# Hybrid layers of a two-block network on one core: output turned in another chunk order and partly inside the last projection, entry splits placed ahead of the norms, roots in place of log and exp

## The chip, the cores and the metric

One NeuronCore of a Trainium2 chip runs the whole program in a single launch. The metric is device time in microseconds, the median of several executions. The same program is timed before and after the change on the same inputs. Engine names are those of the profile: PE is TensorE (PEld its weight loads), DVE VectorE, ACT ScalarE, SP the engine whose queue issues the weight DMAs.

## The reference

Two blocks of two layers each, on 256 tokens of width 2048, in fp32. The first block (a pool and convolution mixer, then a gated linear recurrence) is the same before and after. The change is in the second block, whose layer is, cut to what matters here:

```python
h = rms_norm_2(x, pre_w)
proj = h @ w_in                                  # 2048 -> 5952 columns
a_q, a_k, a_v, a_g, b_q, b_k, b_v, b_g, c_q, c_kv, c_kr, c_g = jnp.split(proj, offsets, axis=-1)
...
y_a = diff_attention(qa, ka, va, lam, subln_w, lam_init)       # 4 heads, each normalised (subln_w)
...
y_b = sliding_window_attention(qb, kb, vb, sinks)              # 16 heads of 64, 2 key heads
...
qc = (rms_norm_2(c_q, q_norm_w) @ w_uq).reshape(B, S, MLA_HEADS, MLA_NOPE_DIM + MLA_ROPE_DIM)
...
kvc = (rms_norm_2(c_kv, kv_norm_w) @ w_ukv).reshape(B, S, MLA_HEADS, MLA_NOPE_DIM + MLA_V_DIM)
...
y_c = causal_attention(qc, kc, vc, (MLA_NOPE_DIM + MLA_ROPE_DIM) ** -0.5)
y = jnp.concatenate([y_a, y_b, y_c], axis=-1) * jax.nn.silu(jnp.concatenate([a_g, b_g, c_g], axis=-1))
out = y @ w_out
return x + rms_norm_2(out, post_w)
```

y has 2048 columns: 512 of y_a, 1024 of y_b, 512 of y_c. `c_q` and `c_kv` (the ranks) are normalised over their 512 columns before the second projection.

## The kernel before

**Weights and splits.** Every fp32 product is made as three fp32r matmuls (`three`): high x high, high x low, low x high. Weights come in chunks of 1 MB (four k-tiles of 128 rows by 512 columns) that SP loads into four `raw` buffers in program order. For each half chunk ScalarE writes the high part (`hi`, line 577, `wh`) and VectorE the low part (`lo`, line 1794, `wl`); there are two `wh`/`wl` slots, so a half chunk can be split once TensorE has used the half two chunks earlier (`s_used`). TensorE waits for the low part (`s_lo`) at each half.

**Entry of a hybrid layer** (`enter` on ACT and DVE, `enter_project` on PE). x is normalised only by a scale per token (`rsh`) that is applied later. Chunks 0 and 1 are multiplied per token tile while the second tile is turned, then chunk 2 and chunk 3 follow. On ACT the order around it is: high parts of h, chunk 2, the square of token tile 0 (`x_square`, lines 953 and 954), chunk 3, the square of tile 1, six DMAs of small parameters (lines 986 to 988), chunk 4. On DVE it is: low parts, chunk 2, low parts, a reciprocal of `rsh` and the scaled rotary tables, chunk 3.

**Projection.** 16 blocks (`BLOCKS`) make 52 chunks, that is half chunks i = 4 to 103 in the loops of all three engines. The table `AFTER` says after which half chunk each further step runs: `move` takes a finished block out of its two PSUM banks (0, 1 or 2, 3 in turn), `norm` turns and scales the rank blocks cq and ckv, `turn` transposes rotated heads, and `score`, `flip`, `weigh` are the attention of one of 14 pairs (2 of kind m for c, 8 of kind b, 4 heads of kind a). A half chunk is 12 matmuls. Each engine walks the table in its own order; DVE does kind a's `weigh` two half chunks late, ACT one.
- `move cq` and `move ckv` (ACT lines 1006 to 1009): square both tiles with accumulation, copy the block, then `Ln` and `Exp` of the sums give the root's inverse; DVE (line 2453) makes scaled diagonals for `norm`.
- `move ag`, `move cg`: ACT writes the sigmoid (line 1027), DVE the product (lines 2493 to 2498).
- `weigh` of kind a: ACT squares (1070), `Ln` and `Exp` (1072, 1073); DVE scales and gates (2576, 2580).

**Turning y and the output projection.** y (`Yt`, tokens in partitions) is turned by `turn_y(g)`, four transposes for a pair g of 128-column tiles into one of banks 4 to 7 (line 1758). ACT copies the pair to `hTh` (1102), DVE subtracts for `hTl` (2626), which frees the bank. After the last half chunk PE turns pairs 0 to 3, and pairs 4 to 7 ahead of k = 0, 2, 4, 6 of output block 0 (`y_ahead`). An output block n has four chunks c (k-tiles 4c to 4c+3), two token tiles, so 24 matmuls a chunk; blocks use banks 0, 1 and 2, 3 in turn. Pairs 0 and 1 hold the a heads, 2 to 5 the b heads, 6 and 7 the c heads, which need the cg product. After the last turned pair ACT issues the DMA of the post-norm row and four of the residual (lines 1108, 726), and DVE waits for that row before it splits output chunk 2.

Of the kernel before, what the change touches and what calls it, by code (L numbers as in the profile page):

```python
# [7 lines left out]
F32 = mybir.dt.float32  # L8
# [6 lines left out]
P = 128  # L15
# [204 lines left out]
for _h, _name in ((48, "bg0"), (56, "bq1"), (64, "bg1"), (72, "aq"), (80, "ak"), (88, "av"), (96, "ag")):  # L220
    AFTER.setdefault(_h, []).append(f"move {_name}")
# [4 lines left out]
YT = KT // 2  # L226
TWO_PI = 6.283185307179586
# [6 lines left out]
def first_block_and_hybrid(nc, a):  # L234

    ctx = ExitStack()
    with ctx:
# [231 lines left out]
        def _(sp):  # L469
# [69 lines left out]
            for L in range(2):  # L539
# [16 lines left out]
                for i in range(16):  # L556
                    ch = st.chunk("hyb", L, NPROJ + i)
                    load(ch, [(slot4(ch), one(layer(w_out2[:, i % 4], L)[:, :, :, (i // 4) * BLK:(i // 4 + 1) * BLK]))])
# [8 lines left out]
        def _(act):  # L567
# [374 lines left out]
            def enter(L, last, SQ):  # L942
# [27 lines left out]
                hyb_split(L, 2)  # L970
                x_square(0)
                hyb_split(L, 3)
# [7 lines left out]
            def hyb_layer(L):  # L980
# [4 lines left out]
                for i, n in enumerate(("q1", "k1", "q2", "k2")):  # L985
                    act.dma_start(LQ[:, i, :], a[f"diff_lambda_{n}_2"][bass.ds(L, 1), :].rearrange("o n -> (o n)").partition_broadcast(P)).then_inc(s_lp, 16)
                act.dma_start(SUB, a["diff_subln_w_2"][bass.ds(L, 1), :].rearrange("o n -> (o n)").partition_broadcast(P)).then_inc(s_lp, 16)
                act.dma_start(SNK, a["sink_logits_2"][bass.ds(L, 1), :].rearrange("o n -> (o n)").partition_broadcast(P)).then_inc(s_lp, 16)
                act.wait_ge(s_save, L * 32 + 64)

# [8 lines left out]
                def move(name, i):  # L999
                    b, _ = done(i)  # L1000
                    if name in ("cq", "ckv"):
# [6 lines left out]
                        step(nc.scalar.activation(qrs[:, 2 * v:2 * v + 2], qss[:, 2 * v:2 * v + 2], ACT.Ln, scale=1.0 / 512, bias=eps)).done()  # L1008
                        nc.scalar.activation(qrs[:, 2 * v:2 * v + 2], qrs[:, 2 * v:2 * v + 2], ACT.Exp, scale=-0.5).then_inc(s_qs, 1)
# [10 lines left out]
                    elif name[1] == "g":  # L1020
# [7 lines left out]
                        ins.then_inc(s_gx, 1)  # L1028

# [35 lines left out]
                def weigh(n):  # L1065
                    kind, h = PAIRS[n]
                    if kind == "a":
# [4 lines left out]
                        step(nc.scalar.activation(ors, oss, ACT.Ln, scale=1.0 / P, bias=C("eps")[:, 1:2])).done()  # L1072
                        nc.scalar.activation(ors, ors, ACT.Exp, scale=-0.5).then_inc(s_os, 1)
# [16 lines left out]

                hyb_split(L, 4, (0,))
                for i in range(6, 2 * NPROJ):
# [6 lines left out]
                hi(st.chunk("hyb", L, NPROJ))  # L1099
                for g in range(YT):  # L1100
                    act.wait_ge(s_yt, count(YT, g + 1))
                    nc.scalar.activation(hTh[:, 2 * g:2 * g + 2, 0:SEQ], ps[:, 4 + g % 4, :].rearrange("p (a b) -> p a b", a=2),
                                         ACT.Copy).then_inc(s_yth, 1)
                    if g == 3:
                        hi(st.chunk("hyb", L, NPROJ + 1))
# [5 lines left out]
                for m in range(2, 16):  # L1111
# [16 lines left out]
        def _(pe):  # L1128
# [160 lines left out]
            def out_block(chunks, T, bank, before=None, after=None):  # L1289

                for c, ch in enumerate(chunks):
                    for t in range(4):
                        if t % 2 == 0:
                            pe.wait_ge(s_lo, ch.half(t // 2))
                        k = 4 * c + t
                        if before:
                            before(k)
                        for m in range(T):
# [3 lines left out]
                                        k == 0, k == KT - 1, False)  # L1302
# [297 lines left out]
            def hyb_layer(L):  # L1600
# [137 lines left out]

                enter_project(L)
# [11 lines left out]
                def turn_y(g):  # L1751
# [932 lines left out]
```

## Time and profile before

| | us |
|---|---|
| median of 3 runs | 2792.46 |
| lowest, highest | 2789.76, 2798.06 |
| the profiled execution: its own time | 2791.23 |
| its span on the core | 2789.4 |

The mean granted clock of TensorE over the span is 0.989 of full speed. The hybrid layers run from about 1877 us to the end: the first layer's entry at 1877 to 1908, its last score at 2205, its output projection to 2341, then the second layer in the same form. In the tables of the profile, a line "[x <-ENGINE ...]" gives the idle time of the instruction's engine just before it and the instruction that ended the wait. Matmul ends are modelled, so starts are the safer reading.

### The profile page before, as it was taken

What the parts mean: (1) busy time and instruction counts of PE and PEld (TensorE: products, weight loads), DVE (VectorE), ACT (ScalarE), POOL (GpSimd) and SP (SyncE); (2) the same over time, 40 slices, a digit from 0 to 9 for tenths busy, and PEclk for the clock granted to TensorE, in tenths of its full rate; (3) what the DMA queues carried; (4) which work ended last, traced back from release to release, by engine and by line L of the source; (5) the groups of instructions that cost most, each with busy time, mean ns of one, the idle gap of its engine ahead of it and who ended that gap; (6) DMA issues with size and microseconds to landing.
All of it is one profiled execution on the core that took longest, in us unless ns stands there. A gap on an engine that the chain in (4) does not pass through costs nothing.

```text
span 2789.4 us, 36467 instructions
## 1 busy us (share of the span) xinstructions
PE 2668.9 (96%) x13605; PEld 2199.2 (79%) x13605; DVE 1898.5 (68%) x2677; ACT 1273.1 (46%) x2017; POOL 0.2 (0%) x4
## 2 busy tenths in 40 slices
PE   5999999999999899999999999998999989999988
PEld 2667778888788788888888888777888777878867
DVE  5765577887887677677677677856566555656654
ACT  6653321222322755345345345456455646545563
POOL 0000000000000000000000000000000000000000
PEclk9999999999999999999999999999999999999999
DMA  8764455665556333323323323455644465544453
GB/s 309 263 223 154 158 168 156 211 197 168 179 211 203 122 97 101 113 87 101 113 87 101 113 86 107 146 172 177 188 133 154 136 207 183 172 151 151 151 181 136
DMA packets 406588, 437.16 MB, mean 157 GB/s; under 512 B 22718, under 2 KB 286536, under 8 KB 404936
## 3 DMA queue, kind: packets, MB, share of 16 engines
q1 hardware_dynamic: 397760, 408.99, 45.9%
q10 hardware_dynamic: 8712, 26.59, 2.6%
q8 instruction: 76, 1.25, 0.2%
q14 instruction: 40, 0.33, 0.0%
HBM read 427.14 MB, written 8.39 MB: 156 GB/s over the span
## 4 chain that ended last, share of the span: by engine, by line
PE 82%; DVE 9%; ACT 5%; issue 2%; DMA 1%; ACTq 0%; DVEq 0%; SPq 0%
PE ps L1132 14%; PE ps L1133 14%; PE ps L1134 14%; PE ps L1135 9%; PE ps L1137 9%; PE ps L1136 9%; DVE wl L1794 3%; DVE acc L1865 2%; ACT wh L577 1%; PE ps L1442 1%; PE ps L1156 1%; PE ps L1158 1%; PE ps L1463 1%; PE ps L1447 1%; PE ps L1735 1%
## 5 line engine op out<-in xcount | busy, mean ns | idle before, releaser
L1794 DVE TENSOR_TENSOR wl<-raw,wh 128x1024 fp32r<-128x1024 f32 (+2 forms) x784 | 821.3, 1077 | 465.4 <-ACT wh L577 453.6
L577 ACT ACTIVATE wh<-raw 128x1024 fp32r<-128x1024 f32 (+2 forms) x784 | 714.4, 943 | 828.2 <-PE ps L1134 472.3
L1132 PE MATMUL ps<-hTh,wh 128*128 128x512 f32 (+1 forms) x2124 | 777.9, 366 | 19.6 <-DVE wl L1794 16.1
L1133 PE MATMUL ps<-hTl,wh 128*128 128x512 f32 (+1 forms) x2124 | 766.8, 361 | 0.0
L1134 PE MATMUL ps<-hTh,wl 128*128 128x512 f32 (+1 forms) x2124 | 765.6, 360 | 0.0
L1135 PE MATMUL ps<-wh,hTh 128*128 128x512 f32 (+1 forms) x1440 | 575.6, 400 | 25.3 <-DVE wl L1794 18.8
L1137 PE MATMUL ps<-wh,hTl 128*128 128x512 f32 (+1 forms) x1440 | 558.5, 388 | 0.0
L1136 PE MATMUL ps<-wl,hTh 128*128 128x512 f32 (+1 forms) x1440 | 557.7, 387 | 0.0
L1132 PEld LDWEIGHTS ps<-hTh,wh 128*128 128x128 f32 x2124 | 401.9, 189 | 89.9 <-DVE wl L1794 9.8
L1133 PEld LDWEIGHTS ps<-hTl,wh 128*128 128x128 f32 x2124 | 401.8, 189 | 61.6 <-issue 0.5
L1134 PEld LDWEIGHTS ps<-hTh,wl 128*128 128x128 f32 x2124 | 401.0, 189 | 62.0
L1135 PEld LDWEIGHTS ps<-wh,hTh 128*128 128x128 f32 x1440 | 272.8, 189 | 88.3 <-DVE wl L1794 26.7
L1137 PEld LDWEIGHTS ps<-wh,hTl 128*128 128x128 f32 x1440 | 272.3, 189 | 55.9
L1136 PEld LDWEIGHTS ps<-wl,hTh 128*128 128x128 f32 x1440 | 273.3, 190 | 51.2 <-issue 1.7
L1865 DVE SCALAR_TENSOR_TENSOR acc<-raw,small,acc 128x1024 f32<-128x1024 f32 x180 | 217.4, 1276 | 0.0
L1053 ACT ACTIVATE arena<-arena,small 128x256 f32<-128x256 f32 (+1 forms) x112 | 49.6, 444 | 128.9 <-DVE small L2537 69.5
L2253 DVE RECIPROCAL arena<-arena 128x512 f32<-128x512 f32 x32 | 107.0, 3345 | 0.0
L1156 PE MATMUL ps<-wh,s 128*66 128x512 f32 x192 | 84.5, 440 | 23.2 <-DVE wl L1794 17.8
L1158 PE MATMUL ps<-wl,s 128*66 128x512 f32 x192 | 81.1, 422 | 0.0
L2288 DVE SCALAR_TENSOR_TENSOR arena<-arena,small,ps 128x128 f32<-128x128 f32 x192 | 66.8, 348 | 6.9
L1156 PEld LDWEIGHTS ps<-wh,s 128*66 128x66 f32 x192 | 28.4, 148 | 52.6 <-DVE wl L1794 19.0
L2281 DVE COPY arena<-ps 128x128 f32<-128x128 f32 x32 | 9.2, 287 | 76.0 <-PE ps L1442 76.0
(296 smaller groups left out, 2029.2 us busy)
## 6 DMA issues: line engine op xcount, KB each, us to landing
raw<-in_ada_w_dram SPq DMA_DIRECT2D x96, 1024.0 KB, 5.3
raw<-in_w_in_dram SPq DMA_DIRECT2D x88, 1024.0 KB, 5.1
raw<-in_od_w_in_dram SPq DMA_DIRECT2D x256, 320.0 KB, 3.5
raw<-in_ev_w_in_dram SPq DMA_DIRECT2D x192, 256.0 KB, 3.9
raw<-in_w_out_dram SPq DMA_DIRECT2D x32, 1024.0 KB, 5.0
raw<-in_ev_w_out_dram SPq DMA_DIRECT2D x16, 1024.0 KB, 5.1
raw<-in_od_w_out_dram SPq DMA_DIRECT2D x16, 1024.0 KB, 5.1
x_save<-arena ACTq DMA_DIRECT2D x6, 1024.0 KB, 5.5
```

What stands on the lines that cost most here:

```text
L577: nc.scalar.activation(wh[:, ch.spl, part], raw[:, ch.raw, part], ACT.Copy).then_inc(s_hi, 1)
L1132: nc.tensor.matmul(out, w_h, x_h, start=first, stop=False, skip_group_check=True)
L1133: nc.tensor.matmul(out, w_h, x_l, start=False, stop=False, skip_group_check=True)
L1134: return nc.tensor.matmul(out, w_l, x_h, start=False, stop=last, skip_group_check=True)
L1135: nc.tensor.matmul(out, x_h, w_h, start=first, stop=False, skip_group_check=True)
L1136: nc.tensor.matmul(out, x_h, w_l, start=False, stop=False, skip_group_check=True)
L1137: return nc.tensor.matmul(out, x_l, w_h, start=False, stop=last, skip_group_check=True)
L1156: nc.tensor.matmul(psA(n), s4[:, 4 * k:4 * k + MS], wh[:, ch.spl, t * BLK:(t + 1) * BLK], start=(k == 0), stop=False, skip_group_check=True)
L1158: ins = nc.tensor.matmul(psA(n), s4[:, 4 * k:4 * k + MS], wl[:, ch.spl, t * BLK:(t + 1) * BLK], start=False, stop=(k == KT - 1), skip_grou ...
L1794: nc.vector.tensor_tensor(wl[:, ch.spl, part], raw[:, ch.raw, part], wh[:, ch.spl, part].bitcast(F32), ALU.subtract).then_inc(s_lo, 1)
L1865: ins = nc.vector.scalar_tensor_tensor(out=acc[:, v, :], in0=w, scalar=silc[:, k:k + 1], in1=acc[:, v, :], op0=ALU.mult, op1=ALU.add)
L2253: step(nc.vector.reciprocal(R[:, d, :], R[:, d, :])).done()
```

## The change

All of it is in the two hybrid layers.
- **Order of y.** Output block 0 takes its chunks in the order `Y_ORDER` = 1, 2, 0, 3 (b heads, b heads, a heads, c heads); SP loads them in that order. `Y_PAIR` and `Y_BANK` give the pair and the bank of the n-th turn. Turn 0 runs after half chunk 101, turn 1 after 102, turns 2 to 7 ahead of k-steps 1, 2, 4, 5, 7, 8 of output block 0 (`Y_AT`). ACT and DVE take their parts of turn 0 inside the loop, and split output chunk 2 ahead of turns 6 and 7. DVE's wait for the post-norm row moves from chunk 2 to behind the split of chunk 5.
- **Gate ag** moves after half chunk 98 (ACT) and 99 (DVE), not 96.
- **Entry.** Both halves of chunk 3 are split ahead of both squares on ACT and ahead of the reciprocal on DVE; the six parameter DMAs and the wait for the saved x come behind the first half of chunk 4.
- **Roots.** `Ln` and `Exp` become one `Sqrt` on ACT and a reciprocal on DVE, for the ranks and for the a heads. For the ranks the root runs one half chunk later (`root`), DVE's part two half chunks later.

```diff
-for _h, _name in (..., (96, "ag")):
+for _h, _name in (..., (98, "ag")):
...
+Y_ORDER = (1, 2, 0, 3)
+Y_PAIR = [2 * c + h for c in Y_ORDER for h in range(2)]
+Y_BANK = (7, 6, 4, 5)
+Y_AT = {1: 2, 2: 3, 4: 4, 5: 5, 7: 6, 8: 7}
...
@@ ACT, enter
                 hyb_split(L, 2)
+                hyb_split(L, 3)
                 x_square(0)
-                hyb_split(L, 3)
                 x_square(1).then_inc(s_sqp, 1)
...
@@ ACT, hyb_layer
-                        step(nc.scalar.activation(qrs[:, 2 * v:2 * v + 2], qss[:, 2 * v:2 * v + 2], ACT.Ln, scale=1.0 / 512, bias=eps)).done()
-                        nc.scalar.activation(qrs[:, 2 * v:2 * v + 2], qrs[:, 2 * v:2 * v + 2], ACT.Exp, scale=-0.5).then_inc(s_qs, 1)
...
+                def root(v):
+                    nc.scalar.activation(qrs[:, 2 * v:2 * v + 2], qss[:, 2 * v:2 * v + 2], ACT.Sqrt, scale=1.0 / 512, bias=eps).then_inc(s_qs, 1)
...
-                        step(nc.scalar.activation(ors, oss, ACT.Ln, scale=1.0 / P, bias=C("eps")[:, 1:2])).done()
-                        nc.scalar.activation(ors, ors, ACT.Exp, scale=-0.5).then_inc(s_os, 1)
+                        nc.scalar.activation(ors, oss, ACT.Sqrt, scale=1.0 / P, bias=C("eps")[:, 1:2]).then_inc(s_os, 1)
...
+                    if i in (8, 16):
+                        root(i // 8 - 1)
...
@@ PE, hyb_layer
+                def turn_y(n):
+                    g = Y_PAIR[n]
+                    if n == 0:
+                        pe.wait_ge(s_45, count(len(USE45), USE45.index("weigh 9") + 1))
+                        pe.wait_ge(s_67, count(len(USE67), USE67.index("turn ak") + 1))
+                    elif n == 1:
+                        pe.wait_ge(s_67, count(len(USE67), len(USE67)))
+                    elif n == 2:
+                        pe.wait_ge(s_45, count(len(USE45), len(USE45)))
+                    elif n == 6:
+                        moved("cg")
+                    if n >= 4:
+                        pe.wait_ge(s_ytl, count(YT, n - 3))
...
+                    if i == 2 * NPROJ - 3:
+                        turn_y(0)
+                    if i == 2 * NPROJ - 2:
+                        turn_y(1)
...
@@ DVE, enter
+                split(3)
                 dve.wait_ge(s_sqp, L * 9 + 25)
                 step(nc.vector.reciprocal(rsh, rsh)).done()
...
                 dve.wait_ge(s_rsh, L + 1)
-                split(3)
...
@@ DVE, hyb_layer
+                        step(nc.vector.reciprocal(qrs[:, 2 * v:2 * v + 2], qrs[:, 2 * v:2 * v + 2])).done()
...
+                        step(nc.vector.reciprocal(ors, ors)).done()
...
+                    for what, late in (("move cq", 2), ("move ckv", 2), ("move ag", 1)):
+                        if what in AFTER.get(i - late, []):
+                            move(what.split()[1], (i - late - 1) // 2)
...
+                    if i == 2 * NPROJ - 3:
+                        lo(st.chunk("hyb", L, NPROJ))
+                        low_turned(0)
+                low_turned(1)
                 lo(st.chunk("hyb", L, NPROJ + 1))
-                for g in range(4, 6):
-                    low_turned(g)
+                low_turned(2)
+                low_turned(3)
                 after(2 * NPROJ - 1)
-                for g in range(6, YT):
-                    low_turned(g)
-                dve.wait_ge(s_gl, L * 16 + 16)
-                for m in range(2, 18):
+                low_turned(4)
+                low_turned(5)
+                lo(st.chunk("hyb", L, NPROJ + 2))
+                low_turned(6)
+                low_turned(7)
+                for m in range(3, 18):
...
+                        if n == 0:
+                            dve.wait_ge(s_gl, L * 16 + 16)
```

ACT at a hybrid layer's entry, before; line 577 is a half chunk's high part, 953 a square.

```order
L577 ACTIVATE wh<-raw 128x1024 x2
L953 ACTIVATE arena,small<-arena 128x2048
L954 ACTIVATE small<-small,cst 128x1
L577 ACTIVATE wh<-raw 128x1024 x2
L953 ACTIVATE arena,small<-arena 128x2048
L954 ACTIVATE small<-small,cst 128x1
```

The same place in the change (577 is now 581, 953 is 957).

```order
L581 ACTIVATE wh<-raw 128x1024 x4
L957 ACTIVATE arena,small<-arena 128x2048
L958 ACTIVATE small<-small,cst 128x1
L957 ACTIVATE arena,small<-arena 128x2048
L958 ACTIVATE small<-small,cst 128x1
L581 ACTIVATE wh<-raw 128x1024
```

Chunk 3's two halves have moved ahead of both squares, and the parameter DMAs that followed the second square now follow one half of chunk 4.

DVE from the ag product to the last score and on, before; 1794 is a half chunk's low part, 2493 to 2498 the product, 2524 and 2526 the read of the last score, 2576 the weighing.

```order
L2576 SCALAR_TENSOR_TENSOR arena<-ps,small 128x128 x2
L2493 SCALAR_TENSOR_TENSOR arena<-ps,small,arena 128x512 x2
L2497 COPY arena<-arena 128x2x256
L2498 TENSOR_TENSOR arena<-arena 128x2x256
L1794 TENSOR_TENSOR wl<-raw,wh 128x1024
L2524 SCALAR_TENSOR_TENSOR arena<-ps,cst 128x2x256
L2526 SCALAR_TENSOR_TENSOR arena<-ps,cst 128x2x128
```

And in the change (1794 is now 1823, 2493 is 2523, 2524 is 2554, 2576 is 2607, 2603 the new reciprocal).

```order
L2607 SCALAR_TENSOR_TENSOR arena<-ps,small 128x128 x2
L1823 TENSOR_TENSOR wl<-raw,wh 128x1024
L2554 SCALAR_TENSOR_TENSOR arena<-ps,cst 128x2x256
L2556 SCALAR_TENSOR_TENSOR arena<-ps,cst 128x2x128
...
L1823 TENSOR_TENSOR wl<-raw,wh 128x1024
L2523 SCALAR_TENSOR_TENSOR arena<-ps,small,arena 128x512 x2
L2527 COPY arena<-arena 128x2x256
L2528 TENSOR_TENSOR arena<-arena 128x2x256
L1823 TENSOR_TENSOR wl<-raw,wh 128x1024
L2603 RECIPROCAL small<-small 128x2
L2607 SCALAR_TENSOR_TENSOR arena<-ps,small 128x128
```

The read of the last score has moved ahead of the product, and the product now stands directly ahead of the weighing of head 2.

PE's turns (line 1758) and their waits, before; each `x3` or `x15` row completes a turn.

```order
L1758 MATMUL ps<-cst,arena 128x128 [waits block_moved0,banks67_read,banks45_read]
L1758 MATMUL ps<-cst,arena 128x128 x15
L1758 MATMUL ps<-cst,arena 128x128 [waits y_turned_low,low_ready]
L1758 MATMUL ps<-cst,arena 128x128 x3
L1135 MATMUL ps<-wh,hTh 128x512 [waits y_turned_low]
```

In the change (1758 is now 1775, 1735 is 1755, 1135 is 1155); the first two turns stand on either side of the last head's weighing.

```order
L1775 MATMUL ps<-cst,arena 128x128 [waits banks67_read,banks45_read]
L1775 MATMUL ps<-cst,arena 128x128 x3
L1155 MATMUL ps<-wh,hTh 128x512 [waits low_ready]
...
L1755 MATMUL ps<-arena 128x128 [waits block_moved1,banks67_read,banks45_read]
...
L1775 MATMUL ps<-cst,arena 128x128 [waits banks67_read]
L1775 MATMUL ps<-cst,arena 128x128 x3
L1155 MATMUL ps<-wh,hTh 128x512 [waits low_ready]
...
L1155 MATMUL ps<-wh,hTh 128x512 [waits y_turned_low,low_ready,block_moved0]
...
L1775 MATMUL ps<-cst,arena 128x128 [waits banks45_read]
```

Matmuls stand between the turns, where the 16 transposes stood in one piece before.

## Rows read from the trace of the kernel before

**Rows 1.** page, part 1: busy time, share of the span, instructions
```profile
PE 2668.9 (96%) x13605; PEld 2199.2 (79%) x13605; DVE 1898.5 (68%) x2677; ACT 1273.1 (46%) x2017; POOL 0.2 (0%) x4
```

**Rows 2.** windows view: span; busy us (count) of PE, PEld, DVE, ACT, POOL; clock, DMA
```profile
1905.10:1923.30 18.20, 18.17 (x73) 14.69 (x74) 8.98 (x16) 12.10 (x17) 0.00 (x0) 0.91 0.41 120
2204.90:2267.70 62.80, 50.47 (x223) 40.41 (x224) 33.55 (x48) 33.37 (x54) 0.00 (x0) 0.92 0.50 174
2657.90:2716.30 58.40, 47.05 (x223) 37.94 (x224) 33.55 (x48) 33.38 (x54) 0.00 (x0) 0.97 0.53 186
```

**Rows 3.** timeline of PE, first hybrid layer's turn: start, us, instruction, [idle before <-releaser]
```profile
2210.73 0.49 PE L1735 MATMUL ps<-arena 128*128 128x128 f32 x2 [1.89 <-DVE arena L2526]
...
2230.46 1.97 PE L1758 MATMUL ps<-cst,arena 128*128 128x128 f32 x16 [2.49 <-DVE arena L2580]
2235.68 0.88 PE L1758 MATMUL ps<-cst,arena 128*128 128x128 f32 x4 [3.25 <-DVE hTl L2626]
...
2245.16 0.63 PE L1758 MATMUL ps<-cst,arena 128*128 128x128 f32 x4 [1.29 <-issue]
...
2255.13 0.50 PE L1135 MATMUL ps<-wh,hTh 128*128 128x512 f32 x1 [3.38 <-DVE wl L1794]
```

**Rows 4.** timeline of PE, second hybrid layer's turn
```profile
2663.74 0.49 PE L1735 MATMUL ps<-arena 128*128 128x128 f32 x2 [1.93 <-DVE arena L2526]
...
2682.59 0.44 PE L1758 MATMUL ps<-cst,arena 128*128 128x128 f32 x2 [2.49 <-DVE arena L2580]
...
2687.81 0.63 PE L1758 MATMUL ps<-cst,arena 128*128 128x128 f32 x4 [1.94 <-DVE hTl L2626]
...
2695.68 0.52 PE L1758 MATMUL ps<-cst,arena 128*128 128x128 f32 x3 [1.28 <-issue]
...
2705.37 0.51 PE L1135 MATMUL ps<-wh,hTh 128*128 128x512 f32 x1 [3.11 <-DVE wl L1794]
```

**Rows 5.** timeline of PE: matmuls at either clock, and four transposes between matmuls
```profile
2212.77 0.63 PE L1136 MATMUL ps<-wl,hTh 128*128 128x512 f32 x1
...
2240.05 0.40 PE L1136 MATMUL ps<-wl,hTh 128*128 128x512 f32 x1
2240.28 0.40 PE L1137 MATMUL ps<-wh,hTl 128*128 128x512 f32 x1
2240.52 0.60 PE L1758 MATMUL ps<-cst,arena 128*128 128x128 f32 x4
2240.88 0.48 PE L1135 MATMUL ps<-wh,hTh 128*128 128x512 f32 x1
```

**Rows 6.** timeline of PE, entry and block kvr of the first hybrid layer
```profile
1905.13 0.80 PE L1135 MATMUL ps<-wh,hTh 128*128 128x512 f32 x1 [2.45 <-DVE wl L1794]
...
1943.43 0.41 PE L1135 MATMUL ps<-wh,hTh 128*128 128x320 f32 x1 [2.07 <-DVE wl L1794]
```

**Rows 7.** timeline of ACT, first hybrid layer's entry
```profile
1896.28 2.09 ACT L953 ACTIVATE arena<-arena 128x2048 f32<-128x2048 f32 x1
...
1898.69 1.99 ACT L577 ACTIVATE wh<-raw 128x1024 fp32r<-128x1024 f32 x2
...
1905.50 1.06 ACT L577 ACTIVATE wh<-raw 128x1024 fp32r<-128x1024 f32 x1 [2.60 <-issue]
```

**Rows 8.** timeline of ACT, block ckv of the first hybrid layer
```profile
1938.78 1.28 ACT L1008 ACT_TABLE_LOAD   x1
...
1941.79 0.72 ACT L577 ACTIVATE wh<-raw 128x640 fp32r<-128x640 f32 x1
```

**Rows 9.** timeline of DVE, first hybrid layer's turn
```profile
2206.14 0.75 DVE L2493 SCALAR_TENSOR_TENSOR arena<-ps,small,arena 128x512 f32<-128x512 f32 x1 [1.27 <-ACT arena L1027]
...
2209.67 0.68 DVE L2524 SCALAR_TENSOR_TENSOR arena<-ps,cst 128x512 f32<-128x512 f32 x1
...
2239.51 0.68 DVE L2626 TENSOR_TENSOR hTl<-ps,hTh 128x512 fp32r<-128x512 f32 x1
...
2253.85 4.63 DVE L1794 TENSOR_TENSOR wl<-raw,wh 128x1024 fp32r<-128x1024 f32 x4 [3.50 <-DMA arena<-in_post_norm_w_dram]
```

More of the change, by code:

```diff
@@ L557, in _ @@
                     ch = st.chunk("hyb", L, NPROJ + i)
-                    load(ch, [(slot4(ch), one(layer(w_out2[:, i % 4], L)[:, :, :, (i // 4) * BLK:(i // 4 + 1) * BLK]))])
+                    load(ch, [(slot4(ch), one(layer(w_out2[:, Y_ORDER[i] if i < 4 else i % 4], L)[:, :, :, (i // 4) * BLK:(i // 4 + 1) * BLK]))])
             for u in range(4):
@@ L1098, in hyb_layer @@
                     after(i)
[L1099 to L1105, printed above, removed]
+                    if i == 2 * NPROJ - 3:
+                        hi(st.chunk("hyb", L, NPROJ))
+                        high_turned(0)
+                high_turned(1)
+                hi(st.chunk("hyb", L, NPROJ + 1))
+                high_turned(2)
+                high_turned(3)
+                after(2 * NPROJ - 1)
+                high_turned(4)
+                high_turned(5)
+                hi(st.chunk("hyb", L, NPROJ + 2))
+                high_turned(6)
+                high_turned(7)
                 act.wait_ge(s_yt, count(YT, YT))
@@ L1110, in hyb_layer @@
                     load_x(u, x_rows, XBN)
-                for m in range(2, 16):
+                for m in range(3, 16):
                     hi(st.chunk("hyb", L, NPROJ + m))
@@ L1287, in gate_rows, with out_block @@
                 nc.tensor.matmul(ps[:, 6 + r % 2, :], ones, gate_block(r), start=True, stop=True).then_inc(s_gb, 1)
-            def out_block(chunks, T, bank, before=None, after=None):
+            def out_block(chunks, T, bank, before=None, after=None, order=range(4)):
                 for c, ch in enumerate(chunks):
@@ L1294, in out_block @@
                             pe.wait_ge(s_lo, ch.half(t // 2))
-                        k = 4 * c + t
+                        k = 4 * order[c] + t
                         if before:
-                            before(k)
+                            before(4 * c + t)
                         for m in range(T):
@@ L1777, in hyb_layer @@
                         free_banks(L * 3 + 6, n)
-                    out_block([st.chunk("hyb", L, NPROJ + 4 * n + c) for c in range(2 if n == 3 else 4)], 2, 2 * (n % 2), y_ahead if n == 0 else None)
+                    out_block([st.chunk("hyb", L, NPROJ + 4 * n + c) for c in range(2 if n == 3 else 4)], 2, 2 * (n % 2), y_ahead if n == 0 else None, order=range(4) if n else Y_ORDER)
                 last_chunks([st.chunk("hyb", L, NPROJ + 14), st.chunk("hyb", L, NPROJ + 15)], 1 if L == 0 else None)
@@ L2602, in after @@
                         if verb == "move":
-                            move(arg, (i - 1) // 2)
+                            if arg not in ("cq", "ckv", "ag"):
+                                move(arg, (i - 1) // 2)
                         elif verb == "norm":
```

67 lines of the change are left out of this document (32 added, 35 removed).

## The prediction

> **What bounds the kernel now.** I read four views in this order. The page's busy times say which engine the span follows: TensorE is busy for 2668.9 of 2789.4 us, VectorE and ScalarE for 68% and 46% [rows 1]. So only time in which TensorE stands still, or runs at the lower clock, can be won; shorter work on ScalarE or VectorE is worth nothing unless TensorE waits for it. The TensorE timeline then gives each wait inside the two hybrid layers, with the instruction that ended it [rows 3, 4, 6]. The windows view sums the stretches around those waits [rows 2]; it holds exactly the same 223 TensorE instructions in both layers. The timelines of ScalarE and VectorE say what was in front of the late instruction [rows 7 to 9]. Everything before the first hybrid layer is untouched and costs or gives nothing.
>
> In the stretch from the last score to the end of output block 0 (I call it the turn), TensorE waited 1.89 + 2.49 + 3.25 + 1.29 + 3.38 = 12.30 us in the first layer [rows 3] and 1.93 + 2.49 + 1.94 + 1.28 + 3.11 = 10.75 us in the second [rows 4]. At the start of each layer it waited 2.45 us for chunk 3 of the entry and 2.07 us in block kvr [rows 6]; the second layer shows the same two waits with the same lengths.
>
> The clock comes on top. A 512-column matmul takes 0.40 us at the upper level, 2.4 GHz, where the next follows after 0.23 us, and 0.63 us at the lower, 1.2 GHz [rows 5]. The granted clock was 0.92 and 0.97 over the two turns and 0.91 over the 18.20 us behind the first entry's wait [rows 2]. The share missing from 1 is time lost: 0.08 x 62.80 = 5.0 us, 0.03 x 58.40 = 1.8 us, 0.09 x 18.20 = 1.6 us. The last is one stretch, so a stretch costs about 1.6 to 1.7 us and the first turn held three.
>
> **Entry.** Chunk 3's high split on ScalarE began at 1898.69, behind a square of 2.41 us that began at 1896.28 [rows 7]; its low split on VectorE stood behind a reciprocal that needs the second square, done at 1905.50 - 2.60 = 1902.90. Both now go first. The high split can start at about 1896.3 and both halves end at 1898.3; VectorE then has 4.4 us for its own part (1.16 us a half, a quarter of 4.63 [rows 9]) and eight small low parts until TensorE wants it at 1905.13 - 2.45 = 1902.68. I take the 2.45 us as gone. Late next is chunk 4: two squares take ScalarE to 1903.1, half a chunk to 1904.1, the six DMA issues with their waits 2.60 us, the second half to 1907.7, its low part to 1908.9. TensorE wants it 36 matmuls of 0.23 us after 1902.68, at 1911.0. Slack 2.1 us; without that cover it would cost what the squares cost, 2.4 us.
>
> **Ranks.** In block ckv, ScalarE loaded a table for Ln, ran it, loaded one for Exp, ran it, and only then split a half chunk of kvr: 1938.78 to 1941.79, 3.01 us [rows 8]. The change runs the square root after that split, so the split comes 3.0 us earlier against a wait of 2.07: gone. What is late next is the normalisation's diagonal, which now stands behind a square root with one load of 1.28 us, a reciprocal and one more VectorE step; by the same durations it ends within 0.3 us of when TensorE wants it, and I keep 0.3 us a layer for it. The rows show a load before Ln and one before Exp. The Trainium skill's page "ScalarE: Activation LUTs", section "Table sets", says the opposite for the old pair and speaks against the new one: Ln and Exp share a set (one load), Exp and Sqrt do not (two). By that rule the old pair was the cheaper, and the ckv gain would be 1.3 us a layer smaller. The rows decide, and rows 8 have both loads. Per attention head of kind a the old code had two loads (Ln, Exp) and the new one has two (Sqrt, Exp), but one of them now falls where ScalarE waits for the row maximum: no cost on TensorE, counted as nothing. The reciprocals added on VectorE (six a layer, a few elements each) are hidden by its 32% idle time.
>
> **Gate ag.** VectorE began the ag product at 2206.14 and could read the last score only at 2209.67 [rows 9]; TensorE's weighing of head 2 waited 1.89 us for that read [rows 3]. Two or three half chunks later the product no longer stands there, and the read can come up to 3.5 us earlier. The wait goes. In its place the read of head 2's weighing becomes late, behind the product; I keep 0.5 us a layer.
>
> **Turns.** Before, 16 transposes stood behind the last head, then each trip (copy on ScalarE, 0.68 us subtraction on VectorE [rows 9], transposes into the freed bank) was seen: 2.49 + 3.25 + 1.29 us. Now pairs 0 and 1 are turned while 24 matmuls of the last projection (5.5 us) are still to come, and each later pair at least three k-steps, 18 matmuls or 4.1 us, before its use. Eight turns of four transposes stay in TensorE's stream at 0.36 us each, from 2240.52 to 2240.88 [rows 5]. The wait of 3.38 us ended with the arrival of the post-norm row, for which VectorE waited 3.50 us before splitting output chunk 2 [rows 9]; that wait now stands behind chunk 5. Next late is chunk 3: after the last turn ScalarE has a copy, five DMA issues (about the 2.60 us of rows 7) and a half split, VectorE 1.16 us, in all some 5.4 us against 24 matmuls of 0.23, 5.5 us. Just covered. The order of chunks and of their loads changes no size and no count.
>
> **Sum.** From below, a turn gives its waits and its clock: 12.30 + 5.0 = 17.3 us and 10.75 + 1.8 = 12.5 us. From above, the stretch at full pace is 168 matmuls of 0.23, 8 turns of 0.36 and 23 small matmuls of about 0.09, that is 38.6 + 2.9 + 2.1 = 43.6 us; 62.80 - 43.6 = 19.2 and 58.40 - 43.6 = 14.8 us. I take the middle, 18.2 and 13.7, less 0.5 each: 17.7 + 13.2 = 30.9 us. Entries and ranks: 2 x (2.45 + 2.07) + 1.6 - 0.6 = 10.1 us. Together 41 us. The profiled execution took 2791.2 us (1.8 around its span) and stands 1.2 us under the median: 2791.2 - 41 + 1.2 = **2751.4 us**.
>
> **Rivals.**
> - Cover too thin at the third output chunk, **chance 0.17**. VectorE's 33.55 us of work in the turn then fill 33.55 / 45.1 = 74% of it, with the product of cg and the last pairs in one queue. If the 3.38 and 3.11 us come back, each with one stretch at the lower clock, 6.5 + 3.4 = 9.9 us of the gain stay out: 2761. For it speaks the slack of under 0.5 us; against it that the arrival which made the wait is no longer waited for.
> - The clock still falls although the waits are gone, **0.08**: 8.4 us back, 2760. Against it: the second layer had waits of 1.28 to 3.11 us and lost only 1.8 us.
> - Turning drops the clock, **0.04**. A mechanism of this kernel: each of 16 turned pairs is followed by one stretch of 1.7 us loss, 27 us, 2779. The matmuls on both sides of the transposes at 2240.52 are at the upper level [rows 5], which speaks against it. The Trainium skill's "TensorE: Matmul & The Clock Gate", Part 4, says that transposes do not count as activity in the way matmuls do; by that rule spreading them into the stream could invite this.
> - The trip is seen eight times instead of once, **0.02**. If ScalarE or VectorE reach each pair so late that the 3.25 us of rows 3 stand before every use, that is 16 x 3.25 = 52 us against the 23 us of waits before, with no clock won: 29 - 10 = 19 us slower, 2811. It turns into a loss from (23 + 10) / 16 = 2.1 us per pair on. Against it: 4.1 us of matmuls between turn and use.
> - The entry's moves only push the wait from chunk 3 to chunk 4 or 5, **0.05**: 10 us of gain gone, 2761.
>
> **How the numbers follow.** My case has 0.64, with its own range 2744 to 2757: its lower end is the upper bounds (19.2 + 14.8 + 10.7 = 44.7 us), the small waits for heads that I left alone and the 2.7 us by which runs fall under the median. The range of 8 in 10 reaches up over the three rivals near 2761 with their spread of runs: 2743 to 2767. A measurement tells 0.3%, 8.4 us, from no change. Every case named but the slower one ends faster by more than that; I give up 0.03 of theirs for what I have not thought of: faster 0.95, within 0.3% 0.03, slower 0.02.
>
> **What would show it.** In the changed profile, TensorE's waits at the two entries' chunk 3, in block kvr, before the head 2 weighing, before the turns and before the third output chunk should each be under 0.6 us; the granted clock over the turn should be 1.00 and the turn 45 us long in both layers; ScalarE should show ten table loads fewer in the hybrid layers. I am wrong if a wait over 1 us stands at chunk 4 or 5 of the entry, at the ckv diagonal, at the weighing of head 3, or at output chunk 3, or if the clock is under 0.97 in the turn.

## The result, and the profile after

The changed kernel takes **2746.06 us** (median of 4 runs, 2743.45 to 2747.09); the kernel before took 2795.01 us beside it (4 runs, 2789.76 to 2798.06). The ratio is 0.983, 95% interval 0.9814 to 0.9846: faster. A second comparison gave 2746.35 us and 0.9828 (0.9813 to 0.9843). The forecast was 2751.4 us in a range of 2743 to 2767: inside the range, with 5.3 us too small a gain. That counts from the 2792.46 us before the change; the runs of the kernel before beside it lie 2.6 us higher.

The busy times of the page, in the columns of [rows 1]:

```profile
PE 2656.7 (97%) x13605; PEld 2194.6 (80%) x13605; DVE 1900.9 (69%) x2689; ACT 1258.7 (46%) x1995; POOL 0.2 (0%) x4
```

The count of TensorE's instructions is the same, and it is busy 12.2 us less although it does the same work. Most of that is time at the lower clock that has gone (in the clock record about 8.5 us in the hybrid layers and 1.7 us ahead of them); the rest I can't place, since a matmul's busy time is modelled. The span fell by 44.1 us, from 2789.4 to 2745.3.

The windows of after are from the first entry to the last score of the first layer, then the two turns; the last two answer to the turns in [rows 2]:

```profile
1877.30:2198.10 320.80, 316.42 (x1658) 262.77 (x1656) 206.56 (x371) 178.28 (x323) 0.00 (x0) 1.00 0.51 162
2198.13:2242.80 44.67, 44.67 (x224) 37.14 (x224) 32.60 (x50) 28.73 (x49) 0.00 (x0) 1.00 0.56 198
2627.60:2672.30 44.70, 44.70 (x225) 37.18 (x225) 32.57 (x50) 28.65 (x49) 0.00 (x0) 1.00 0.55 200
```

Both turns are 44.7 us at a clock of 1.00, with TensorE busy from end to end: 62.80 - 44.67 = 18.1 us and 58.40 - 44.70 = 13.7 us won, 31.8 in all.

The waits view of TensorE over the two hybrid layers (engine, line, waited for: us in total, times, longest), first of the kernel before, from 1876 us on:

```profile
PE ps L1135 <- DVE wl L1794: 17.5, 8, 3.4
PE ps L1735 <- DVE arena L2526: 5.8, 6, 1.9
PE ps L1758 <- DVE hTl L2626: 5.2, 2, 3.2
PE ps L1758 <- DVE arena L2580: 5.0, 2, 2.5
PE ps L1758 <- issue: 2.6, 2, 1.3
PE ps L1135 <- DVE hTl L2377: 2.3, 2, 1.1
```

and all that this view shows of the changed kernel, from 1877 us on:

```profile
PE ps L1155 <- DVE hTl L2406: 2.3, 2, 1.1
PE ps L1755 <- DVE arena L2556: 2.0, 4, 0.5
PE ps L1155 <- DVE wl L1823: 1.9, 2, 1.0
PE ps L1575 <- DVE arena L2169: 1.7, 4, 0.5
PE ps L1690 <- DVE arena L2483: 0.5, 2, 0.2
PE ps L1741 <- DVE small L2578: 0.4, 2, 0.2
```

Before, with the smaller groups of that view, the waits are 42 us; after, 8.8 us. The three groups of line 1758, the turns' own, are gone entirely, and of the eight waits for a weight split two are left, 0.96 and 0.98 us at chunk 2 of each entry. The rest of the gain is the clock: before, five stretches at the lower clock stood in the hybrid layers (one in the first entry, three in the first turn, one in the second), each of 3.4 us in the record and, by the terms of the prediction, worth about 1.7 us; after, there is none. (Both kernels have one more behind their last matmul, where it costs TensorE nothing.) 33.4 + 5 x 1.7 = 41.9 us. The hybrid layers (from their first transposes to the end of the span, called the **hybrid part** below) went from 912.5 to 867.9 us, that is 44.6. The missing 2.7 us I don't have one by one; a wait's length is counted from the modelled end of the matmul ahead, 0.40 us after its start, while at full pace the next begins after 0.23 us [rows 5], and 18 fewer waits (34 before, 16 after) at up to 0.17 us each are room enough for it.

### The profile page after: what moved, and what is told of

Its sections match the earlier page's. It is cut to its first block, busy times and chain, and to the rows that moved or that the text cites. A ratio compares the mean times of both kernels' runs of the same rounds, so it can differ in the third digit from the quotient of the medians.

```text
span 2745.3 us, 36471 instructions
## 1 busy us (share of the span) xinstructions
PE 2656.7 (97%) x13605; PEld 2194.6 (80%) x13605; DVE 1900.9 (69%) x2689; ACT 1258.7 (46%) x1995; POOL 0.2 (0%) x4
## 4 chain that ended last, share of the span: by engine, by line
PE 85%; DVE 8%; ACT 3%; issue 2%; DMA 1%; ACTq 0%; DVEq 0%; SPq 0%
PE ps L1152 14%; PE ps L1153 14%; PE ps L1154 14%; PE ps L1155 10%; PE ps L1157 10%; PE ps L1156 10%; DVE wl L1823 3%; DVE acc L1894 2%; PE ps L1462 1%; PE ps L1176 1%; PE ps L1178 1%; PE ps L1483 1%; ACT wh L581 1%; PE ps L1755 1%; PE ps L1467 1%
```

## The experiments

Each edit is against the changed kernel, except the first. The number I compare is the hybrid part of the profiled execution, since what stands ahead of it is the same code and still took from 1875.2 to 1878.3 us in these profiles, and 1881.4 us in one. The changed kernel has 867.9 us in both of its profiles, the kernel before 912.5 in its only one. Where stretches at the lower clock fall in the hybrid layers the number holds for that execution alone, by steps of 1.7 us: the runs of the kernel before spread from 2786.91 to 2799.64 us with clocks of 0.985 to 0.991, those of the changed kernel from 2743.45 to 2747.09 us.

### The entry alone, in the kernel before

```diff
                 hyb_split(L, 2)
-                x_square(0)
                 hyb_split(L, 3)
+                x_square(0)
                 x_square(1).then_inc(s_sqp, 1)
...
+                split(3)
                 dve.wait_ge(s_sqp, L * 9 + 25)
...
                 dve.wait_ge(s_rsh, L + 1)
-                split(3)
```

> The kernel before with only the entry's order changed: chunk 3 split ahead of both squares on ScalarE and ahead of the reciprocal on VectorE; the six parameter DMAs stay where they were. Theory (each wait is worth its own length, and nothing takes its place): the 2.45 us wait for chunk 3 is gone in both layers and with it the lower-clock stretch behind the first, so 2 x 2.45 + 1.6 = 6.5 us less than before, and the 2.07 us in block kvr stays. Rival (the wait only moves): a wait of 1 to 2.5 us appears at chunk 4 or 5, because the squares and the DMA issues (2.60 us) now stand directly ahead of chunk 4, and the total is within 2 us of before.

Measured: 2788.54 us, ratio 0.9985 (0.9975 to 0.9995); hybrid part 910.1, 2.4 us less than before. By this pair of profiles it is **a miss** for my theory; the medians of 10 and 13 runs say 4.2 us (by the interval 1.4 to 7.0), which leaves the 6.5 us open. Both waits of 2.45 us are gone, but 0.44 and 0.46 us came at the first half of chunk 4 (the squares and, in this kernel, the parameter DMAs too stand ahead of it), so the sum of waits fell by 4.35 us and not by 4.9. And this profile has six lower stretches, where that of before has five. The timeline of TensorE at block kvr of the first hybrid layer, before:

```profile
1943.68 0.31 PE L1136 MATMUL ps<-wl,hTh 128*128 128x320 f32 x1
1943.82 0.31 PE L1137 MATMUL ps<-wh,hTl 128*128 128x320 f32 x1
1943.97 0.31 PE L1135 MATMUL ps<-wh,hTh 128*128 128x320 f32 x1
```

The wait ahead of them is 2.07 us [rows 6]. In this experiment it is 2.07 us too, and the windows view of the 9 us behind it, first and second hybrid layer, is:

```profile
1938.31:1947.31 9.00, 9.00 (x54) 9.00 (x55) 5.54 (x12) 4.00 (x8) 0.00 (x0) 0.81 0.71 235
2386.80:2395.80 9.00, 9.00 (x54) 9.00 (x55) 5.60 (x12) 4.06 (x9) 0.00 (x0) 0.81 0.71 233
```

The same 9 us before:

```profile
1943.43:1952.43 9.00, 9.00 (x65) 9.00 (x66) 7.14 (x14) 5.08 (x9) 0.00 (x0) 1.00 0.69 236
```

So the wait of 2.07 us, which cost nothing beyond its length in the profile of before, cost 0.19 x 9 = 1.7 us more in either layer here. The stretch in the first entry is gone, and the turns have four between them, so the balance is one more: 4.35 - 1.7 = 2.65 us is what is left, against 2.4 in the hybrid part. That the removed wait moved the stretch onto the next is not shown. With one profile of each kernel, another execution of the same kernel could have shown it elsewhere; the next experiment has such a case within one program.

### The entry as before, in the changed kernel

```diff
                 hyb_split(L, 2)
-                hyb_split(L, 3)
                 x_square(0)
+                hyb_split(L, 3)
...
-                hyb_split(L, 4, (0,))
...
                 act.wait_ge(s_save, L * 32 + 64)
+                hyb_split(L, 4, (0,))
...
-                split(3)
                 dve.wait_ge(s_sqp, L * 9 + 25)
...
                 dve.wait_ge(s_rsh, L + 1)
+                split(3)
```

> The changed kernel with the entry's order as before (chunk 3 behind the first square on ScalarE and behind the reciprocal on VectorE, the six parameter DMAs ahead of chunk 4); turns, gate and roots as changed. In the kernel before, the same edit alone gave only about 2 us over the hybrid layers where 6.5 were expected, because lower-clock stretches fell elsewhere. Theory (a wait is worth its length, and the clock comes on top by chance): 2.45 us of wait twice, and one lower-clock stretch or none or two: 4.9 to 8.2 us over the changed kernel. Rival (the entry's order is worth only the 2 us that its run alone showed): under 3 us over.

Measured: 2752.75 us, 0.9852 (0.9835 to 0.987); hybrid part 875.1, 7.2 us over the changed kernel's profile beside it, within the 4.9 to 8.2 expected; the medians, 2752.75 and 2746.35, differ by 6.4. The waits of 2.45 and 2.46 us are back. TensorE behind each of them, windows view:

```profile
1903.46:1912.46 9.00, 9.00 (x39) 7.43 (x40) 4.66 (x4) 6.19 (x9) 0.00 (x0) 1.00 0.66 205
2335.77:2344.77 9.00, 9.00 (x33) 7.30 (x34) 4.67 (x4) 4.67 (x8) 0.00 (x0) 0.82 0.64 206
```

Practically the same wait in the same program: once the clock stays at 2.4 GHz, once it falls to 1.2 GHz for a stretch. In the kernel before, the same wait of 2.45 us was followed by a stretch in the first layer and by none in the second. So a stretch belongs to no wait for good. The entry is worth 6 to 7 us in the changed kernel; in the kernel before it gave 2.4 us by the profiles and 4.2 us by the medians, and these don't tell whether it is worth less there.

### The turns and output chunks as before

```diff
-Y_ORDER = (1, 2, 0, 3)
+Y_ORDER = (0, 1, 2, 3)
...
-Y_BANK = (7, 6, 4, 5)
+Y_BANK = (4, 5, 6, 7)
...
                 moved("ag")
+                for g in range(4):
+                    turn_y(g)
```

(with ACT's and DVE's parts, the loads and the wait for the post-norm row back in their old places; entry, roots and gate stay changed)

> The changed kernel with y turned as before (natural chunk order, 16 transposes behind the last projection, the wait for the post-norm row ahead of output chunk 2); entry, roots and gate ag as changed. Theory: the waits 2.49 + 3.25 + 1.29 + 3.38 us come back in the first layer and 2.49 + 1.94 + 1.28 + 3.11 us in the second, some shorter by the 1.3 us of a table load that the last head no longer has, with one to three lower-clock stretches of 1.7 us: 18 to 24 us over the changed kernel. Rival (the gain of the turn comes from the roots and gate ag, which put the last head earlier): under 8 us over the changed kernel.

Measured: 2772.0 us, 0.9931 (0.9912 to 0.9949); hybrid part 892.1, 24.2 us over the changed kernel, at the upper end of the 18 to 24 expected. The waits come back at the trip and at the third output chunk, in the timeline of TensorE:

```profile
2223.44 1.09 PE L1772 MATMUL ps<-cst,arena 128*128 128x128 f32 x4 [3.54 <-DVE hTl L2653]
...
2232.83 0.63 PE L1772 MATMUL ps<-cst,arena 128*128 128x128 f32 x4 [1.29 <-issue]
...
2242.54 0.50 PE L1149 MATMUL ps<-wh,hTh 128*128 128x512 f32 x1 [3.12 <-DVE wl L1808]
```

The second layer has the same three, 3.54, 1.29 and 2.89 us. These are 15.7 us of waits. The clock is low four times, once for twice the usual length, so as long as in five stretches: 15.7 + 5 x 1.7 = 24.2. The wait of 2.49 us behind the last head [rows 3], which I also expected, did not come back; what removed it I did not try apart. The turns and the output chunks carry more than half of the whole gain, and nothing of the ag wait is in it.

### The order of chunks without the overlap

```diff
-                    if i == 2 * NPROJ - 3:
-                        turn_y(0)
-                    if i == 2 * NPROJ - 2:
-                        turn_y(1)
...
+                turn_y(0)
+                turn_y(1)
                 moved("ag")
```

(ACT's and DVE's parts of turn 0 likewise come behind the loop)

> The changed kernel with turns 0 and 1 behind the last half chunk instead of inside the last projection; the chunk order 1, 2, 0, 3 and the later turns stay. Theory (two things make the turn free: chunk order, which takes the last head and gate cg off the path, and the overlap, which hides the first trip): one trip shows per layer, ScalarE 0.6 and VectorE 0.7 us for a pair and the queues ahead of them, 2 to 4 us a layer, 4 to 8 us in all, with at most one lower-clock stretch a layer more. Rival (order alone does it): under 1 us. Rival (overlap alone does it): over 15 us.

Measured: 2749.3 us, 0.9844 (0.9828 to 0.9861); hybrid part 870.6, only 2.6 us over the changed kernel where 4 to 8 were expected: **a miss in size**. There is one new wait a layer, and no lower stretch:

```profile
2218.32 1.04 PE L1775 MATMUL ps<-cst,arena 128*128 128x128 f32 x8
2220.43 0.47 PE L1155 MATMUL ps<-wh,hTh 128*128 128x512 f32 x1 [1.07 <-DVE hTl L2652]
```

So of the 24.2 us of the run above, the two turns inside the last projection carry 2.6. The other 21.6 go to what this kernel keeps: the new order of chunks (b heads first, whose y is ready before the last head), the turns spread between k-steps, the third output chunk split ahead of the last pairs, and the moved wait for the row, of which only the last was tried by itself, below.

### The wait for the post-norm row back

```diff
                 low_turned(7)
+                dve.wait_ge(s_gl, L * 16 + 16)
                 for m in range(3, 18):
...
-                        if n == 0:
-                            dve.wait_ge(s_gl, L * 16 + 16)
```

> The changed kernel with VectorE's wait for the post-norm row back directly behind the last turn, ahead of output chunk 3 (it stood behind chunk 5). Theory (the row arrives 4.8 us after its issue, some 1.2 us after the split could begin): a wait of 0.7 to 1.3 us at output chunk 3 in each layer, none elsewhere, 1.4 to 2.6 us in all. Rival (the arrival was the whole of the 3.38 us before): about 3 us a layer.

Measured: one run of 2752.82 us; hybrid part 875.7, 7.8 us more. **A miss in size**: 1.4 to 2.6 us were expected. VectorE's timeline at the split of the third output chunk, in this kernel:

```profile
2236.96 4.63 DVE L1823 TENSOR_TENSOR wl<-raw,wh 128x1024 fp32r<-128x1024 f32 x4 [5.55 <-DMA arena<-in_post_norm_w_dram]
```

and in the changed kernel:

```profile
2235.81 4.63 DVE L1823 TENSOR_TENSOR wl<-raw,wh 128x1024 fp32r<-128x1024 f32 x4 [2.35 <-ACT wh L581]
```

TensorE waits 2.71 and 2.86 us at that chunk, the second time with a lower stretch (clock 0.81 over the next 9 us). 5.57 + 1.7 = 7.3 of the 7.8 us. That is three times what I had expected, since I reckoned with the landing time of before. The tile view of the row gives this time; before:

```profile
DMA to landing us min/median/max: 4.5/4.7/4.8
```

in this experiment:

```profile
DMA to landing us min/median/max: 6.8/6.9/7.0
```

The changed kernel itself has 6.9 to 7.0 us too, so it is not this edit that made the landing longer. The row is the same transfer in all three; it takes 2.2 us longer to land than before. The kernel before and the changed one differ in what moves beside it (the output chunks' loads now run into it: DMA share of the turn 0.55 and 0.56, before 0.50 and 0.53 [rows 2]); that this is the cause was not tried by itself. Had the change left this wait where it was, most of the 9.9 us of the rival with the third output chunk would have come true.

### How thin the cover at the third output chunk is

```diff
                     load_x(u, x_rows, XBN)
+                for _ in range(6):
+                    step(nc.scalar.activation(small[:, 506:507], eps, ACT.Copy)).done()
                 for m in range(3, 16):
```

> The changed kernel with six chained tiny copies on ScalarE (about 0.2 us each, 1.2 us in all) ahead of output chunk 3's split. Theory (chunk 3 is covered by 0.3 us only): a wait of 0.7 to 1.2 us appears at output chunk 3 in each layer. Rival (the cover is larger than the starts show): no wait.

Measured: one run of 2750.09 us; hybrid part 870.4, 2.4 us more. The timeline of ScalarE and of TensorE in this kernel:

```profile
2235.29 1.38 ACT L1132 ACTIVATE small<-cst 128x1 f32<-128x1 f32 x6 [1.98 <-issue]
2236.70 3.90 ACT L581 ACTIVATE wh<-raw 128x1024 fp32r<-128x1024 f32 x4
```

```profile
2239.07 0.50 PE L1157 MATMUL ps<-wh,hTh 128*128 128x512 f32 x1 [0.92 <-DVE wl L1825]
```

A delay of 1.41 us on ScalarE becomes a wait of 0.92 us in the first layer and 0.89 in the second, within the expected 0.7 to 1.2. The cover was 0.5 us by the recorded waits, 0.2 by the 2.4 / 2 = 1.2 us that it cost: thin, and yet whole.

### Each turn done four times

```diff
-                    for k in range(2):
+                    for k in (0, 1) * 4:
```

> The changed kernel with every turn of y done four times over, 16 transposes a pair instead of 4 (the same result, 96 transposes more a layer). Theory (transposes do not pull the clock down): 16 turns x 12 transposes x 0.09 us = 17 us over the changed kernel, granted clock in the turn 1.00. Rival (transposes do not hold the clock up): lower-clock stretches in the turn as well, granted clock under 0.97 there and over 22 us.

Measured: one run of 2766.87 us; hybrid part 889.7, 21.7 us more, between the 17 us of my theory and the 22 of the rival. The first turn, windows view, and one of its groups of transposes:

```profile
2197.20:2253.00 55.80, 55.77 (x318) 47.91 (x319) 33.14 (x50) 29.96 (x50) 0.00 (x0) 1.00 0.51 182
```

```profile
2227.86 1.91 PE L1775 MATMUL ps<-cst,arena 128*128 128x128 f32 x16
```

With four times the transposes in it the turn still runs at 1.00, and so does the second layer's. The clock decides against the rival that turning drops it; the time is above my 17 us because 192 more transposes for 21.7 us are 0.11 us each, where 4 in 0.36 us [rows 5] had given 0.09. The Trainium skill's "TensorE: Matmul & The Clock Gate", Part 4, says that transposes do not count as activity in the way matmuls do; between matmuls, in groups of up to 16, this run shows no effect of it on the clock.

### Gate ag as before

```diff
-for _h, _name in (..., (98, "ag")):
+for _h, _name in (..., (96, "ag")):
```

(on VectorE, the move is likewise back at its old half chunk)

> The changed kernel with gate ag moved out after half chunk 96 on both engines, as before. Theory: the wait of about 1.9 us for VectorE's read of the last score comes back in both layers, with a lower-clock stretch in none or one of them: 3.8 to 5.5 us over the changed kernel. Rival (with the roots shortened, ScalarE and VectorE reach the score in time anyway): under 1 us over.

Measured: 2749.69 us, 0.9846 (0.9828 to 0.9863); hybrid part 872.3, 4.3 us more, within 3.8 to 5.5, though by other waits than written:

```profile
2202.79 0.71 PE L1755 MATMUL ps<-arena 128*128 128x128 f32 x4 [1.21 <-DVE arena L2556]
...
2209.76 0.52 PE L1741 MATMUL ps<-cst,arena 128*128 128x128 f32 x3 [0.55 <-DVE arena L2586]
```

Before, the first was 1.89 us [rows 3]; here it is 1.21 with the gate in its old place, so 0.7 us of it had already gone with the other edits; which of them I did not try apart. The second is one that the changed kernel doesn't have at this place.

### The roots as Ln and Exp, in their new places

```diff
-                    nc.scalar.activation(qrs[...], qss[...], ACT.Sqrt, scale=1.0 / 512, bias=eps).then_inc(s_qs, 1)
+                    step(nc.scalar.activation(qrs[...], qss[...], ACT.Ln, scale=1.0 / 512, bias=eps)).done()
+                    nc.scalar.activation(qrs[...], qrs[...], ACT.Exp, scale=-0.5).then_inc(s_qs, 1)
```

(the same for the a heads, and without the reciprocals on VectorE)

> The changed kernel with Ln and Exp in place of root and reciprocal, at the new places. Theory (the ranks' gain came from the place behind the split, the attention's table loads are hidden): each ckv normalisation waits 1.3 to 1.8 us on TensorE, and the last head's weighing delays the reads of banks 4 and 5 by up to 1.3 us; 2.5 to 6 us over the changed kernel, ten table loads more. Rival (the loads are the gain): block kvr waits its 2.07 us again and the turn shows waits of over 1.5 us; over 8 us.

Measured: 2755.08 us, 0.9863 (0.9842 to 0.9885); hybrid part 874.6, 6.7 us more, a little over the 2.5 to 6 expected; ScalarE has 38 table loads in the hybrid layers, eight more than the changed kernel and not ten. The timeline of ScalarE in block ckv of this kernel:

```profile
1933.68 1.28 ACT L1028 ACT_TABLE_LOAD   x1
1934.97 0.30 ACT L1028 ACTIVATE small<-small,cst 128x2 f32<-128x2 f32 x1
1935.29 1.28 ACT L1029 ACT_TABLE_LOAD   x1
1936.58 0.20 ACT L1029 ACTIVATE small<-small 128x2 f32<-128x2 f32 x1
```

and in the changed kernel:

```profile
1935.48 1.28 ACT L1028 ACT_TABLE_LOAD   x1
1936.77 0.30 ACT L1028 ACTIVATE small<-small,cst 128x2 f32<-128x2 f32 x1
1936.98 1.98 ACT L581 ACTIVATE wh<-raw 128x640 fp32r<-128x640 f32 x3
```

One more load of 1.28 us stands ahead of the norm's diagonal, and TensorE's wait there is 1.54 instead of 0.23 us, in both layers. The wait in kvr does not come back: the place of the root had removed it, not its form. The remainder are waits of 0.2 to 0.7 us around the last heads. Ln and Exp take a load each here, as they did before. [rows 8] show only the load for Ln of that block; the timeline has the other one too:

```profile
1940.07 0.29 ACT L1008 ACTIVATE small<-small,cst 128x2 f32<-128x2 f32 x1
1940.39 1.28 ACT L1009 ACT_TABLE_LOAD   x1
```

The section "Table sets" of the Trainium skill's "ScalarE: Activation LUTs" has them in one set, and the measurement decides against it here.

### Two waits that were left: chunk 2, and the saved x

What is left in the entry is 1.14 us for the first low part of the second token tile and 0.96 us for chunk 2, both behind ScalarE. First, chunk 2 ahead of the last two high groups:

```diff
-                for i in range(2, 8):
+                for i in range(2, 6):
                     high(i)
                 hyb_split(L, 2)
+                for i in range(6, 8):
+                    high(i)
                 hyb_split(L, 3)
```

> The changed kernel with ScalarE splitting chunk 2 of a hybrid entry ahead of the last two of its eight groups of high parts (it came behind all eight). Theory: the 0.96 and 0.98 us that TensorE still waits for chunk 2 go, 1.9 us less than the changed kernel, and chunk 3 stays covered. Rival: the last high parts, now 1.9 us later, become late for chunk 3 on VectorE, and a wait of up to 1 us appears there: no gain.

Measured: 2745.4 us, 0.9823 (0.9805 to 0.9841); hybrid part 865.4, 2.6 us less than the changed kernel (1.9 expected). The waits of 0.96 and 0.98 us are gone. The medians (2745.4 and 2746.06) don't tell the two kernels apart; the hybrid part and the waits do, in one profile.

Then, on top of it, the issue of the DMAs that save x behind the second tile's first two high groups:

```diff
                 hyb_split(L, 1, (1,))
+                for i in range(2, 4):
+                    high(i)
                 save(XN, L * 4 + 8)
-                for i in range(2, 6):
+                for i in range(4, 6):
                     high(i)
```

> As e6_chunk2_ahead (chunk 2's high part ahead of the last two groups of high parts), and ScalarE also issues the two DMAs that save x behind the second tile's first two groups of high parts instead of ahead of them. Theory (the 1.14 us that TensorE waits for the second tile's first low part is ScalarE's 0.8 us of DMA issue and the wait in front of it): that wait falls to 0.4 us or less in both layers, 1.5 us less than e6 and 4 us less than the changed kernel. Rival (VectorE, not ScalarE, is late there, since it ends the last residual sum just before): the wait stays over 0.9 us and the kernel equals e6.

Measured: **2742.54 us** (5 runs, 2742.03 to 2742.64), 0.9815 (0.9801 to 0.983); hybrid part 862.6, 5.3 us under the changed kernel's 867.9, where 4 were expected. The changed kernel ran beside it at 2746.35 us (2745.4 to 2746.61): their runs don't overlap, and the medians differ by 3.8 us. The waits view of this kernel over the hybrid layers is short:

```profile
PE ps L1759 <- DVE arena L2560: 2.0, 4, 0.5
PE ps L1579 <- DVE arena L2173: 1.8, 4, 0.5
PE ps L1694 <- DVE arena L2487: 0.5, 2, 0.2
PE ps L1745 <- DVE small L2582: 0.4, 2, 0.2
```

Two small moves on ScalarE took the 4.2 us of waits for hTl and chunk 2 away. This version beats both kernels.

## Why the prediction was right, and where it was too small

- **Turns and gate: right.** 18.1 and 13.7 us against 17.7 and 13.2. The turn takes 44.7 us, forecast 45, at a clock of 1.00. All three waits of the turns are gone, and so is the one at the weighing of head 2; the 0.5 us a layer that I kept for a new one there did not appear, which is about the difference. That the turns do carry it is shown by undoing them (+24.2 us) and the gate (+4.3 us).
- **Third output chunk: right, with the margin as thin as said.** "Just covered", 5.4 us against 5.5: the probe found 0.2 to 0.5 us of cover. The gain rests on the wait for the row having moved; in its old place it costs 7.8 us. The reason that I gave, that the arrival "is no longer waited for", held; its price, had it been, I put at 1.4 to 2.6 us ahead of that experiment, too low, because the row takes 2.2 us longer to land than before.
- **Entry and ranks: right by the layer, wrong by the part.** From the first transposes to the ckv norm the layers won 6.3 and 4.9 us, 11.2 against 10.1. Chunk 4 shows no wait, the diagonal waits 0.23 us for the 0.3 that I kept, and kvr's wait is gone. But the entry by itself in the kernel before gave 2.4 us (4.2 by the medians), where the sum's terms for it are 2 x 2.45 + 1.6 = 6.5 us. The weak step is the price of the clock: I tied a stretch of 1.6 us to the entry's wait as if it belonged to it. The runs show that it does not: of two equal waits in one execution one is followed by a stretch and the other is not. So the clock's term of one part cannot be taken by itself. In the whole change it came out right, because every wait over 1.2 us in the hybrid layers went, and in no profile was a wait there as short as those left followed by a stretch. Part of that is luck: the 8.4 us for the clock are what one profile of the kernel before showed, with five stretches, and another execution could have shown more or fewer.
- **The table loads: right.** ScalarE has 30 in the hybrid layers, before 40: ten fewer. I gave [rows 8] as the source for both loads, but of the two they show only one (the other stands in the section on Ln and Exp).
- **The 5.3 us that were missing.** The span fell by 44.1 us for my 41: turns +0.9, entries and ranks +1.1, and 1.6 in the stretches between, among them four waits of up to 0.4 us at line 1713 that are gone; I had no term for those. From it goes 0.5 for the parts ahead of the hybrid layers. The other 2.2 us are no part of the kernel: I put the median 1.2 us above the profiled execution, as it was before, and of the changed kernel it is 1.0 us below (2747.09 and 2746.06).
- **The rivals.** That the clock still falls: no stretch in the hybrid layers after the change. That turning drops it: not so with four times the transposes either, in one profile. The trip seen eight times: no wait at any turn. The wait pushed to chunk 4 or 5: none in the changed kernel, though 0.44 and 0.46 us at chunk 4 where the DMA issues stay ahead of it (the entry alone).

## What to carry to other kernels

A transposition that must make a round trip over two other engines can start with the data that is ready earliest, if the order of the sum allows it, and be spread between the matmuls that follow: here that, with the wait for the row moved and a split put ahead of the last turns, gave all but 2.6 us of the turns' 24; how much each of these gave is not shown, except for the row. A wait on a DMA belongs behind the last work that does not need it, and its landing time can change with the kernel around it: 4.7 us before, 7.0 in the changed kernel. Price waits of 2 to 3 us together with their clock as a set: with all of them removed no stretch was left, while with one removed in either layer the profile had six stretches instead of five.

## What the runs showed of the hardware that I had not expected

- The same wait costs its length or 1.7 us more. Of waits from 1.9 to 3.5 us some are followed by 3.4 us at the lower clock and others are not: 2.45 us not and 2.46 us yes in one execution, 2.07 us not in the profile of before and yes in that of the entry alone. In the hybrid layers none followed a wait of up to 1.55 us. What selects between them these runs don't tell.
- The same row, issued in the same way, took 4.7 us to land in the kernel before and 7.0 in the changed one.
- Transposes of 128 x 128 between matmuls cost 0.09 to 0.11 us each and kept the upper clock, also 16 in a row.
